# Two feed-forward tails turn their normed rows for the stage that follows, and the hybrid stage's opening is put in another order

## What is computed

```
h = x * (1 + scale) + shift                      # scale, shift: rows of silu(c) @ ada_w + ada_b
y = (silu(h @ w_gate) * (h @ w_up)) @ w_down     # feed-forward, hidden width 2816
x = layernorm(ALPHA * x + (1 + gate) * y) * g + b
...
h = x * (1 + scale) + shift                      # attention reads this h, in its layer
proj = h @ w_in
...
h = x * rsqrt(mean(x * x) + 1e-6) * g_norm1 * (1 + scale) + shift      # hybrid reads this h
z = h @ w_in                                     # then split into conv, q, k, v, o, gates
```

## Time and profile before

| | us |
|---|---|
| median of 3 runs | 2736.38 (2735.71 to 2737.82) |
| the profiled execution, its own time | 2738.78 |
| its span | 2737.0 |
| mean granted TensorE clock | 0.968 of full speed |
| busy: TensorE, VectorE, ScalarE, GpSimd | 2538.3, 2035.8, 1067.4, 382.2 |

### The profile page before, as it was taken

The page is one execution under the profiler, slowest core; times in us unless marked ns, Lnnn a source line. Parts: engine busy times, 40 slices in busy tenths (PEclk is TensorE's granted clock), DMA queues, the critical chain, the costliest instruction groups (busy, mean ns, idle before and its releaser), DMA issues. The chain is left out here.

```text
span 2737.0 us, 43084 instructions
## 1 busy us (share of the span) xinstructions
PE 2538.3 (93%) x17291; PEld 2015.3 (74%) x17291; DVE 2035.8 (74%) x2894; ACT 1067.4 (39%) x1425; POOL 382.2 (14%) x207
## 2 busy tenths in 40 slices
PE   5999888889999989998999989999998999999993
PEld 3785888777888844467788867887578788888883
DVE  6872666687777628777877666986746999999994
ACT  2631244522220022543222004333223777777772
POOL 1000000000000020000000000000002356665551
PEclk8999999999999999999999998999998999999997
DMA  6221122336663280205665323321407899999983
GB/s 210 77 87 41 65 80 80 125 112 212 186 190 116 85 273 32 77 32 154 212 187 169 116 78 106 93 79 45 154 1 268 328 372 371 371 369 363 361 302 127
DMA packets 247595, 458.89 MB, mean 168 GB/s; under 512 B 31157, under 2 KB 205917, under 8 KB 232089
## 3 DMA queue, kind: packets, MB, share of 16 engines
q1 hardware_dynamic: 227384, 432.37, 45.4%
q0 software_dynamic: 14384, 24.25, 2.6%
q10 hardware_dynamic: 5682, 0.20, 0.1%
HBM read 456.24 MB, written 30.56 MB: 178 GB/s over the span
## 5 line engine op out<-in xcount | busy, mean ns | idle before, releaser
L49 PE MATMUL ffn_bank<-ffn_xT_high,ffn_wi_high 128*128 128x512 f32 x704 | 275.5, 391 | 5.5 <-DVE stay_z_r L43 3.1
L50 PE MATMUL ffn_bank<-ffn_xT_low,ffn_wi_high 128*128 128x512 f32 x704 | 275.2, 391 | 0.0
L3436 POOL DMA_INDIRECT expert_rows<-exp_ys,exp_to_row x32 | 153.8, 4805 | 45.2 <-issue 44.4
L49 PEld LDWEIGHTS ffn_bank<-ffn_xT_high,ffn_wi_high 128*128 128x128 f32 x704 | 132.5, 188 | 33.6 <-DVE stay_z_r L43 3.9
L50 PEld LDWEIGHTS ffn_bank<-ffn_xT_low,ffn_wi_high 128*128 128x128 f32 x704 | 132.3, 188 | 28.2
L43 DVE TENSOR_TENSOR moe_u_low<-moe_u,exp_u_high 128x4096 fp32r<-128x4096 f32 x32 | 141.6, 4425 | 12.8 <-ACT exp_u_high L3510 12.6
L43 DVE TENSOR_TENSOR moe_g_low<-moe_g,moe_g_high 128x4096 fp32r<-128x4096 f32 x32 | 141.6, 4425 | 8.5 <-ACT moe_g_high L3510 8.2
L43 DVE TENSOR_TENSOR moe_d_low<-moe_d,exp_d_high 128x4096 fp32r<-128x4096 f32 x32 | 141.4, 4419 | 0.0
L51 PE MATMUL ffn_bank<-ffn_xT_high,stay_z_r 128*128 128x512 f32 x352 | 139.8, 397 | 0.0
L51 PE MATMUL ffn_bank<-ffn_wo_high,ffn_act_low 128*128 128x512 f32 x352 | 138.0, 392 | 0.0
L49 PE MATMUL ffn_bank<-ffn_wo_high,ffn_act_high 128*128 128x512 f32 x352 | 137.7, 391 | 0.0
(11 more groups left out here) (730 smaller groups left out, 6726.9 us busy)
## 6 DMA issues: line engine op xcount, KB each, us to landing
moe_g<-in_w_e_gate SPq DMA_DIRECT2D x32, 2048.0 KB, 9.5
moe_u<-in_w_e_up SPq DMA_DIRECT2D x32, 2048.0 KB, 10.0
moe_d<-in_w_e_down SPq DMA_DIRECT2D x32, 2048.0 KB, 9.3
ffn_nw<-in_ada_w SPq DMA_DIRECT2D x24, 1024.0 KB
ffn_nw<-in_w_ada SPq DMA_DIRECT2D x24, 1024.0 KB
stay_z<-in_ffn_w_in SPq DMA_DIRECT2D x44, 512.0 KB, 5.1
ffn_wi<-in_ffn_w_in SPq DMA_DIRECT2D x44, 512.0 KB, 5.2
chunks_ada<-in_ada_w SPq DMA_DIRECT2D x16, 1024.0 KB, 5.3
```

The lines of the kernel that those rows point to most:

```text
L49: nc.tensor.matmul(out, w[0], x[0], start=start, stop=False, **kw)
L50: nc.tensor.matmul(out, w[0], x[1], start=False, stop=False, **kw)
L3436: nc.gpsimd.indirect_dma_start(ys_dram, bass.IndirectOffsetOnAxis(ap=to_row[h][:, 0, 1:2].bitcast(U32), axis=0), ys[h][:, :], None, bounds ...
```

## The change

The feed-forward tail gets a third step. TensorE turns each normed tile with 8 transposes into its own two banks, which the norm has read (`turn`); in `ffn1` it multiplies by a diagonal matrix of the rows' inverse root mean squares instead, so that the norm of hybrid is in the turned rows. ScalarE evicts tiles 0 and 1 and the first half of tile 3 with the next stage's scale and shift, VectorE tile 2 and the other half of tile 3, each as 128 by 128, into `xT`, which the stage no longer reads then. `swiglu` returns `xT`, and `dsa` and `hybrid` read it as `hT`. Both drop their own transposes and evictions. `dsa` issues its three broadcasts behind the bias rows; `hybrid` issues `gt` and `norm_g` after job 8, casts and splits block 0 in halves, lets job 1 follow job 0 by two slices, and puts the small transposes, jobs 2 and 3 and `low(2)` ahead of the gate projection and of the gate chain.

```diff
@@ swiglu, TensorE
+                def turn(t):
+                    pe.wait_ge(s["normed"] if squares is None else s["diag_done"], t + 1)
+                    for k in range(KD):
+                        if squares is None:
+                            last = nc.tensor.transpose(turned_at(t, k), x[:, t, k:D:KD], ident[:, :])
+                        else:
+                            last = nc.tensor.matmul(turned_at(t, k), x[:, t, k:D:KD], diag[:, t, :], start=True, stop=True, skip_group_check=True)
+                        if k % 4 == 3:
+                            last.then_inc(s["turn_psum"], 1)
                 for t, j in ((1, 1), (2, 0), (2, 1), (3, 0), (3, 1)):
+                    if t == LAST and j == 0:
+                        turn(0)
                     for f in range(STEADY, NF):
                         down(f, t, j)
+                for t in range(1, NT):
+                    turn(t)
@@ swiglu, ScalarE
                 for t in range(NT):
                     act.wait_ge(s["var_done"], t + 1)
                     nc.scalar.activation(rstd[:, t:t + 1], mv[:, t, 1:2], ACT.Sqrt).then_inc(s["root"], 1)
+                    if t > 1:
+                        act.wait_ge(s["affine_done"], 1)
+                        take_turned(t - 2, 0, KD)
+                    if squares is not None:
+                        act.wait_ge(s["normed"], t + 1)
+                        if t:
+                            act.wait_ge(s["squared"], t)
+                        col = squares[:, t:t + 1]
+                        nc.scalar.activation(sil[:, :, :].rearrange("p a t -> p (a t)"), x[:, t, :], ACT.Square, accum_out=col).then_inc(s["squared"], 1)
+                        act.wait_ge(s["squared"], t + 1)
+                        act.wait_ge(s["eps_done"], 1)
+                        nc.scalar.activation(col, col, ACT.Sqrt, scale=1.0 / D, bias=stay["eps"][:, :]).then_inc(s["mean_root"], 1)
+                take_turned(LAST, 0, KD // 2)
@@ swiglu, VectorE
+                def diagonal(t):
+                    col = squares[:, t:t + 1]
+                    dve.wait_ge(s["mean_root"], t + 1)
+                    link(nc.vector.reciprocal(col, col))
+                    nc.vector.tensor_scalar(diag[:, t, :], ident[:, :], col, None, ALU.mult).then_inc(s["diag_done"], 1)
+                def between(t):
+                    if squares is not None and t:
+                        diagonal(t - 1)
+                def take_turned(t, first, count):
+                    for k in range(first, first + count):
+                        dve.wait_ge(s["turn_psum"], 2 * t + k // 4 + 1)
+                        nc.vector.tensor_scalar(next_rows(t, k), turned_at(t, k), sc[:, k:k + 1], sh[:, k:k + 1], ALU.mult, ALU.add).then_inc(s["turned"], 1)
                 deepnorm_rows(...
+                              s["var_done"], s["root"], s["normed"], between=between)
+                dve.wait_ge(s["affine_done"], 1)
+                take_turned(LAST - 1, 0, KD)
+                if squares is not None:
+                    diagonal(LAST)
+                take_turned(LAST, KD // 2, KD // 2)
+    return xT
@@ deepnorm_rows, between the variance and the wait for its root
+        if between is not None:
+            between(t)
@@ dsa
-                pool.dma_start(gt[:, :], spread(gate)).then_inc(s["v_loaded"], 16)
...
+                pool.dma_start(gt[:, :], spread(gate)).then_inc(s["tail_loaded"], 16)
...
-                for k in range(KD):
-                    for t in range(NT):
-                        last = nc.tensor.transpose(bank[k][:, t * P:(t + 1) * P], x[:, t, k:D:KD], ident[:, :])
-                    last.then_inc(s["xT_psum"], 1)
-                pe.wait_ge(s["h_done"], KD)
+                keep_busy(nc, bank[6], ident, 24)
                 pe.wait_ge(s["b_loaded"], 32)
@@ hybrid, GpSimd
+                pool.wait_ge(s["job_done"], 8)
+                pool.dma_start(gt[:, :], spread(gate)).then_inc(s["late_loaded"], 16)
+                pool.dma_start(norm_g[:, :], spread(w["m_norm_g"])).then_inc(s["late_loaded"], 16)
@@ hybrid, TensorE
+                keep_busy(nc, bank[5], ident, 36)
+                pe.wait_ge(s["first_low"], 1)
+                for k in range(KD + OPENING):
+                    if k < KD:
+                        pe.wait_ge(s["h_split"], k + 1)
+                        opening(0, k)
+                    if k >= OPENING:
+                        pe.wait_ge(s["wb_split"], 1)
+                        opening(1, k - OPENING)
...
+                for n in range(2, 4):
+                    project(n)
+                pe.wait_ge(s["if_split"], 1)
                 for k in range(KD):
                     last = matmul_halves(nc, bank[4][:, :], (w_if_high[:, k, :], w_if_low[:, k, :]), (hT_high[:, k, :], hT_low[:, k, :]),
...
+                for n in range(4, EARLY - 2):
+                    project(n)
@@ hybrid, VectorE
                 for k in range(KD):
+                    if k == 4:
+                        for n, done in enumerate(("first_high", "wb_highs")):
+                            own = slice(n * P, (n + 1) * P)
+                            dve.wait_ge(s[done], 1)
+                            low_half(nc.vector, wb_low[0][:, :, own], wb[0][:, :, own], wb_high[0][:, :, own]).then_inc(s[("first_low", "wb_split")[n]], 1)
+                    nc.vector.tensor_copy(hT_high[:, k, :], hT[:, k, :]).then_inc(s["h_high"], 1)
+                    dve.wait_ge(s["h_high"], k + 1)
                     low_half(nc.vector, hT_low[:, k, :], hT[:, k, :], hT_high[:, k, :]).then_inc(s["h_split"], 1)
+                low(1)
...
+                low(2)
```

More of the change, by code:

```diff
@@ L2348, with hybrid @@
 LAST_TILES = (2, 3, 0, 1)
-def hybrid(nc, stay, x_in, x_stored, mod, w, upto_dram, pick_dram):
+def hybrid(nc, stay, hT, x_in, x_stored, mod, w, upto_dram, pick_dram):
     gate = mod[2 * D:3 * D]
@@ L2692, in take @@
                         take_high(blk + 2)
-                for n in range(4):
+                for n in range(2):
                     take(n)
+                act.wait_ge(s["if_loaded"], 32)
+                act.wait_ge(s["vec_psum"], 1)
+                nc.scalar.copy(w_if_high[:, :, :], w_if[:, :, :]).then_inc(s["if_high"], 1)
+                for n in range(2, 4):
+                    take(n)
+                act.wait_ge(s["v_loaded"], 16 * 2)
+                act.wait_ge(s["if_psum"], 1)
+                for n, row in enumerate((0, F_ROW)):
+                    nc.scalar.activation(gates[:, n, :], bank[4][row:row + M_HEADS, :], ACT.Identity, bias=bif[:, n:n + 1]).then_inc(s["if_taken"], 1)
+                act.wait_ge(s["abs_done"], 1)
+                nc.scalar.activation(gates[:, 3, :], gates[:, 3, :], ACT.Exp, scale=-1.0).then_inc(s["exp_done"], 1)
+                act.wait_ge(s["exp_done"], 1)
+                nc.scalar.activation(gates[:, 3, :], gates[:, 3, :], ACT.Ln, bias=1.0).then_inc(s["ln_done"], 1)
                 act.wait_ge(s["m_done"], 1)
@@ L2756, in _ @@
                 link(nc.vector.memset(v[:, :, :, M_DIM:M_DIM + 1], 1.0))
-                dve.wait_ge(s["root"], 1)
-                link(nc.vector.reciprocal(ssq[:, :], ssq[:, :]))
-                for t in range(NT):
-                    nc.vector.tensor_scalar(xn[:, t, :], x[:, t, :], ssq[:, t:t + 1], None, ALU.mult).then_inc(s["xn_done"], 1)
                 def low(n):
@@ L3691, in two_blocks @@
         rwkv(nc, stay, a["ffn_w_in"][0], z_loaded[0], a["x"][0], a["c"][0], a["ada_w"][0], a["ada_b"][0], mods[0], w, a["ln_g"][0, 0], a["ln_b"][0, 0], a["ident"], a["masks"], a["head_rows"])
-        swiglu(nc, "ffn0", stay, z_loaded[0], mods[0], a["ffn_w_in"][0], a["ffn_w_out"][0], a["ln_g"][0, 1], a["ln_b"][0, 1], spill[0], spilled[0],
+        turned = swiglu(nc, "ffn0", stay, z_loaded[0], mods[0], a["ffn_w_in"][0], a["ffn_w_out"][0], a["ln_g"][0, 1], a["ln_b"][0, 1], spill[0], spilled[0],
                a["c"][0], a["ada_w"][1], a["ada_b"][1], mods[1])
```

151 lines of the change are left out of this document (58 added, 93 removed).

## The result

The changed kernel took 2748.41 us (median of six runs, 2746.17 to 2756.47), the kernel before on the same chip 2737.69 (six runs, 2735.71 to 2740.86). The ratio is 1.0051 (95% interval 1.0037 to 1.0064): the change is slower, by 10 to 18 us. The prediction said 2737.2 and at most 2743.5.

What follows compares the result with a forecast made beforehand. TensorE, busy 93% of the span, was taken to bound the kernel, so edits help only where it stands still or another engine ends a stage. +3.0 - 1.3 + 5.4 - 6.3 = +0.8 us on 2736.38 gave 2737.2 us, range 2731.0 to 2743.5.

Steps and rivals of the forecast that it cites:

- ffn0 tail: End of ffn0: VectorE's twelve evictions at 0.27 us delay attention's start, other turning hidden; +3.0 us.
- Attention's opening: Start of attention: without transposes and evictions, projections start 6.9 us after the stage began, not 8.2; -1.3 us.
- ffn1 tail: End of ffn1: diagonals, tile 3's turn, evictions and barrier move hybrid's start from 1640.2 to 1645.6; +5.4 us.
- TensorE turning tile 3 by 8 matmuls at an estimated 0.23 us each, 1.8: ffn1's tail: tile 3's turn against the diagonal, at the lower clock level, takes 1.8 us.
- in TensorE's idle time: Feed-forward tail: tiles 1 and 2 are turned while VectorE norms, tile 0 within a 0.5 us slack; nothing lost.
- Between, 0.45: ffn1's tail: reciprocal and diagonal product add 0.15 us x 3 before tile 3 is normed; 0.45 us.
- barrier 1.75: ffn1's end: hybrid starts 1.75 us after VectorE's last eviction.
- Hybrid's opening: Start of hybrid: first matmul 4.2 us sooner, 48 matmuls 2.9 less at full clock, small transposes +0.9; -6.3 us.
- rival 1: Hybrid's and attention's openings: clock falls in the new pauses, 2.9 us in hybrid, about as much in attention; 2743.0; chance 0.22.
- Gate chain: Hybrid, behind the gate projection: TensorE's 2.2 us stall moves to job 6 and is not removed; 0 (-4 to +1).
- stands still once: Hybrid after its opening: TensorE later stands still only once, 2.24 us before job 4.
- Rival 3: Both tails: ScalarE's evictions and TensorE's turning of tile 0 aren't hidden; +1.5 us in each, 2740.2; chance 0.08.

Runs made afterwards that it cites:

- scaled_rows: Changed kernel, but in ffn1's tail VectorE scales the rows and TensorE turns them by transposes, not diagonal products; 1.0049 of the kernel before.
- plain_turn: Changed kernel, but ffn1's tail turns rows by plain transposes, leaving out the division by the root mean square; 1.0034 of the kernel before.
- late_rows: Changed kernel, but ScalarE issues hybrid's six row loads behind its casts of block 0, not ahead; 1.0047 of the kernel before.
- longer_busy: Changed kernel, but 70 and not 36 small matmuls keep TensorE busy in hybrid's opening; 1.0047 of the kernel before.
- order_only: Kernel before, with only hybrid's opening reordered; norm, transposes and evictions stay in hybrid; measured twice, 0.9991 and 1.0001 of the kernel before.
- attention_only: Changed kernel with only the ffn0 and attention part; ffn1's tail and hybrid are those of before; 1.0018 of the kernel before.
- balanced: Changed kernel, but each tail's last sixteen evictions are shared eight and eight between VectorE and ScalarE, not twelve and four; 2751.94 us, measured once.
- order_warm: Kernel before with hybrid's opening reordered, plus 14 small matmuls at the head of TensorE's stream in hybrid; 0.9988 of the kernel before, 2733.59 us.
- hybrid_only: Changed kernel with only the ffn1 and hybrid part; ffn0's tail and attention's opening are those of before; 1.0048 of the kernel before.
- mended: Changed kernel with rows scaled then transposed, row loads behind block 0's casts, evictions shared eight and eight, 54 small matmuls in hybrid's opening; 1.0026 of before.

## Why the prediction was wrong

The direction and the size were missed by two steps: ffn1's tail, 6.5 us over its price, and hybrid's opening, 4.3 us short in its two main terms. Its steps in order:

- **ffn0 tail, +3.0**: right, +3.4. The eviction took 0.33 us in a row of twelve and not 0.27, so 3.91 instead of 3.2; the row of 0.34 was the better price, the discount for overlapping starts, taken from casts and low parts of 512 columns, did not apply. The barrier, 1.55, was 0.2 shorter than assumed.
- **Attention's opening, -1.3**: right, -1.36 (6.82 us against 8.18). That the three broadcasts left the window showed as well: the index weights, foreseen at 20.4, were not waited for.
- **ffn1 tail, +5.4**: this step failed; it was +11.9. By its own terms: *TensorE turning tile 3 by 8 matmuls at an estimated 0.23 us each, 1.8* was 4.27 us of waiting; the rate came from a transpose, and a float32 product is not one. The turning of tiles 0 to 2 was costed at nothing, *in TensorE's idle time*: at 3.85 us a tile it was not, and 1.97 us stood before VectorE's last read (slack 0.5 us, as the prediction said of ffn0) and 1.14 between the evictions of tile 2. *Between, 0.45* was next to nothing: from the first read to the last norm's end it took 27.25 us, and 25.22 before the change plus the 1.97 is 27.19. The twelve evictions were 0.8 over, the *barrier 1.75* was 2.40; 2.4 stood there before the change too, and a row of another stage was taken in its place. Sum of the misses: 2.5 + 2.0 + 1.1 - 0.4 + 0.8 + 0.65 = 6.65, where 11.9 - 5.4 is 6.5. scaled_rows and plain_turn show that the product and its chain make up 8.5 of the 11.9.
- **Hybrid's opening, -6.3**: the first projection came 1.3 us sooner, not 4.2, as block 0 landed at 9.0 instead of the 6.8 that the earlier trace rows has. The prediction counted the small transposes that the change moves (+0.9), but not that the issue of their six row loads moves to the very start, beside block 0. late_rows shows that this costs 2.4 us. The full clock did not come either: 12.57 us for the jobs instead of 11.1, as in rival 1, and for the reason it named, the pause after `keep_busy`; with a pause of 2.67 or 1.40 us (late_rows, longer_busy) the clock stayed at 1.00. In late_rows the step comes out nearly as priced: first projection 3.7 us sooner than before the change, the 48 matmuls in 11.10 instead of 14.06 us, and with the prediction's own +0.9 that is -5.8. So the failed term here is the landing of block 0, and the clock that fell with it. With the norm left in hybrid, the reordering alone (order_only) gained 3.0 us.
- **Gate chain, 0**: right. It stood for 2.29 us before job 6 (2.24 before job 4 in the earlier trace rows), and the matmuls behind it ran slow as before. What the prediction says of the path, that TensorE *stands still once* later, is wrong: from 1850 to 1945 us it waited for VectorE four times already before the change, 8.3 us in all, and which course it takes there moves the time by 2.9 to 4.5 us.
- **Rivals**: rival 1 had its mechanism in hybrid, at 1.5 us and not 2.9, and not in attention, where the clock was 1.00 from 978.5 on. Rival 3, *the turned rows aren't hidden*, was what happened in ffn1's tail, but with a price of 1.5 us where 3.1 us fell to the waits of tiles 0 to 2 alone, and a chance of 0.08. Neither it nor the range had a term for a product that costs more than a transpose, so the range stopped 5 us short.

Adding the parts up: +2.2 for ffn0 and attention, +11.9, -1.3, and the rest of hybrid between -3.1 and -0.4 (399.2 and 396.5 before, 396.1 after), is +10 to +12 us; the times say +10 to +18. Of the -3.1, 2.9 us are the shorter course behind `hyb_wgt` that the changed kernel's profile has and those of before don't (84.5 us against 87.4 and 87.5); without it the parts give +12.5 to +15.3.

## What to carry to other kernels

A matmul of float32 operands and a transpose of the same shape look alike in the program and differ by a factor of nearly four in time: price a product by a product's row, and if there is none in the trace, put four times the transpose in the range. When work moves from the head of a stage to its tail, look at what it had hidden at the head: here the norm and the transposes ran beside the first weights' landing, and ScalarE's square of the last tile held its small loads back by 1.2 us. A reordering and a move that come as one change are worth separating; here the one gained 3 us in the stretches (in time no gain is shown), and the other lost several times as much.

## What the runs showed of the hardware that was not expected

**Small loads on another queue.** Six loads of rows, issued by ScalarE within 2 us, put off the landing of a 1 MB load on SyncE's queue from 6.6 to 9.0 us; 2048 pieces of 16 bytes behind it on its own queue did not. The loads are 0.09 MB; at the end of block 0's landing about one DMA engine's share (0.07) was at work, at 23 GB/s.

**The middle of hybrid has two courses.** The waits that TensorE has from 1850 to 1945 us come in two patterns. Waits of TensorE there (in total, times, longest), the changed kernel, then longer_busy:

```profile
PE hyb_bank L2615 <- DVE stay_z L2937: 3.8, 3, 2.4
PE hyb_bank L2625 <- DVE hyb_wgt L2948: 3.6, 2, 1.8
```

```profile
PE hyb_bank L2615 <- DVE stay_z L2937: 6.7, 2, 4.3
PE hyb_bank L2625 <- DVE hyb_wgt L2948: 1.8, 1, 1.8
```

Every profile has one of the two. Those with a wait of 3.9 to 4.9 us have a granted clock of 0.90 to 0.93 in that stretch (0.95 to 0.97 in the others) and a rest of 396.5 to 401.7 us: before, attention_only, plain_turn, longer_busy, balanced, order_warm. The others have 393.8 to 396.5. From the first wait for `hyb_wgt` to the first product of `hyb_cv` and `hyb_wr` the one group takes 87.4 to 89.0 us and the other 84.5 to 84.8, with nothing between. This is where plain_turn (+4.4 us against the changed kernel), longer_busy (+3.4) and order_warm (+4.4) gave back what they had gained earlier, and where order_only's kernel got 2.9 us that the reordering did not make. What chooses the course was not tried. It need not be the kernel: order_warm's profile is that of the slowest of its executions (2738.40 us, of 2727.28 to 2738.40), longer_busy's too (2754.50), and both have the long course; the changed kernel's, scaled_rows' and late_rows' are those of their fastest, with the short one. So it may change from one execution to the next.

**The clock at attention's start.** In both profiles of order_only's kernel and in that of order_warm, the 32 old transposes at attention's start took 6.2 to 6.6 us instead of 5.06 and the first 64 projections 9.2 to 9.4 instead of 7.7, though nothing ahead of them was edited. TensorE, 8 us from the same point of the stage, before the change, then order_only:

```profile
978.12:986.12 8.00, 8.00 (x68) 1.00 1.02 354
```

```profile
976.47:984.47 8.00, 8.00 (x51) 0.79 1.03 359
```

In hybrid_only, with the same attention code, the transposes and projections took 5.08 and 7.68. It is not the order kernels alone: in mended the 64 projections took 9.09 us, in balanced, equal up to there, 7.68. So after the same pause the clock came back at different times in kernels that are equal up to there, and the middle is 1.6 to 3.4 us longer in order_only's kernel and order_warm than in the kernel before. What decides it is open. Only order_only's kernel was profiled twice, so that it goes with the program, and not with the execution, is not shown.
